# mLSTM: q and k copied with their 64-partition blocks exchanged, each score product split over both 64-row groups and two PSUM banks

## The reference, cut to what matters

```python
s = jnp.exp(d_log - m_t[..., None]) * jnp.einsum('bclhd,bcshd->bchls', qc, kc)
num = jnp.einsum('bchls,bcshv->bclhv', s, vc) + ...
den = jnp.sum(s, axis=-1) + ...
```

## Time and profile before

| what | us |
|---|---|
| runs shown | 3657.66, 3667.47, 3668.46 |
| median of them | 3667.47 |
| the profiled execution, its own time | 3659.06 |
| its span in the trace | 3657.3 |
| first product of layer 0 to the end of its last head | 339.47 to 463.48 |
| first product of layer 1 to the end of its last head | 2279.09 to 2375.73 |

### The profile page before, as it was taken

How to read it: one execution, slowest core, us unless ns; L and a number is a source line. 1 busy time by engine, 2 the same in 40 slices (tenths; PEclk the granted TensorE clock), 3 DMA queues, 4 the chain that set the end, 5 groups by cost and what they waited for, 6 DMA issues and landing times.

```text
span 3657.3 us, 70414 instructions
## 1 busy us (share of the span) xinstructions
PE 3407.7 (93%) x29874; PEld 2310.7 (63%) x29874; DVE 1172.9 (32%) x2555; ACT 707.3 (19%) x1346; POOL 104.0 (3%) x167
## 2 busy tenths in 40 slices
PE   7889999999999999999999989998999999999998
PEld 4456757678765777776777656666677665444444
DVE  1443415335624211111111453425264242222222
ACT  2313312122222100000001432320132201111111
POOL 0000100000000000000000000100000000000000
PEclk9999999999999999999999999998999999999999
DMA  5511020010034999999999401020201269999997
GB/s 214 231 53 52 24 81 12 29 53 30 30 121 173 350 362 374 361 355 364 362 362 356 169 2 66 33 81 12 81 30 56 106 255 410 415 416 416 417 414 292
DMA packets 100570, 733.01 MB, mean 200 GB/s; under 512 B 7888, under 2 KB 14160, under 8 KB 58336
## 3 DMA queue, kind: packets, MB, share of 16 engines
q1 hardware_dynamic: 90512, 692.54, 48.1%
q0 software_dynamic: 9808, 36.75, 3.3%
HBM read 710.34 MB, written 18.92 MB: 199 GB/s over the span
## 4 chain that ended last, share of the span: by engine, by line
PE 69%; DMA 19%; DVE 6%; ACT 3%; issue 2%; DVEq 0%; POOL 0%; SPq 0%; ACTq 0%; POOLq 0%
PE psum L654 14%; DMA ring<-in_w_e_gate 9%; PE psum L1199 8%; PE psum L546 8%; PE psum L1190 6%; DMA ring<-in_w_e_up 5%; PE psum L539 5%; PE psum L1231 4%; PE psum L1052 4%; PE psum L656 3%; DMA ring<-in_w_ada 2%; PE psum L776 2%; PE psum L1237 2%; DVE work L1944 2%; DMA ring<-in_w_e_down 2%
## 5 line engine op out<-in xcount | busy, mean ns | idle before, releaser
L654 PE MATMUL psum<-HT,ring 128*128 128x256 f32 x2560 | 614.9, 395 | 19.9 <-DVEq L2046 8.6
L654 PEld LDWEIGHTS psum<-HT,ring 128*128 128x128 f32 x2560 | 499.2, 198 | 117.1 <-issue 26.4
L1199 PE MATMUL psum<-work,ring 128*64 128x96 f32 x11264 | 486.2, 247 | 45.6 <-issue 30.7
L1199 PEld LDWEIGHTS psum<-work,ring 128*64 128x64 f32 x11264 | 471.1, 137 | 62.6 <-issue 44.7
L1430 ACT ACTIVATE work<-psum,small 128x768 f32<-128x768 f32 (+4 forms) x208 | 146.2, 703 | 700.7 <-PE psum L1237 327.1
L546 PE MATMUL psum<-ring,HT 128*128 128x512 f32 (+1 forms) x768 | 276.0, 521 | 0.0
L1190 PE MATMUL psum<-ring,work 128*64 128x256 f32 x1024 | 244.0, 393 | 30.0 <-DMA ring<-in_w_e_gate 28.1
L1191 PE MATMUL psum<-ring,work 128*64 128x256 f32 (+1 forms) x1024 | 238.0, 372 | 0.0
L1433 ACT ACTIVATE work<-psum 128x256 f32<-128x256 f32 (+7 forms) x219 | 103.5, 473 | 654.2 <-PE psum L546 237.8
L1231 PE MATMUL psum<-ring,work 128*64 128x512 f32 x960 | 220.3, 598 | 6.7 <-DMA ring<-in_w_e_down 6.4
L546 PEld LDWEIGHTS psum<-ring,HT 128*128 128x128 f32 x768 | 145.8, 190 | 127.3 <-issue 120.5
(11 more groups left out here) (229 smaller groups left out, 3791.7 us busy)
## 6 DMA issues: line engine op xcount, KB each, us to landing
ring<-in_w_e_gate SPq DMA_DIRECT2D x64, 2048.0 KB, 13.0
ring<-in_w_e_up SPq DMA_DIRECT2D x48, 2048.0 KB
ring<-in_w_e_down SPq DMA_DIRECT2D x48, 2048.0 KB
ring<-in_w_ada SPq DMA_DIRECT2D x24, 2048.0 KB, 11.7
ring<-in_w_e_up SPq DMA_DIRECT2D x32, 1536.0 KB, 11.0
ring<-in_w_gate SPq DMA_DIRECT2D x16, 2048.0 KB, 8.2
HT<-in_w_e_up SPq DMA_DIRECT2D x16, 2048.0 KB
ring<-in_w_e_gate SPq DMA_DIRECT2D x16, 1536.0 KB
```

Source lines behind the costliest of these rows:

```text
L654: pe.matmul(b[:, 0:256], w[:, k, d4 * P:(d4 + 1) * P], HT[:, k, off:off + 256], start=(k == 0), stop=(k == KD - 1))
L1199: ins = pe.matmul(b[lo:lo + 64, f * cap:(f + 1) * cap], w[:, k, c0:c0 + 64], e_xs[:, k, 0:cap], start=(k == 0), stop=(k == KD - 1))
```

## The change

`swap_head` copies, by two DMAs from POOL's queue for each head, the keys of a head and the last 384 columns of its queries into the other 64 partitions of a free area: for head 0 before the row copies, for heads 1 and 2 after the mask of item (0, 5), for head 3 after the mask of item (2, 1). `products` splits each item's queries into two halves. The first half uses the head's own row group; the second uses the exchanged copy in the other row group, except for items (0,0), (1,0), (3,0) and (3,1), where the copy is not used and both halves run in the own row group. Each half takes a bank of ring "d", which gets bank 2 (3, 4, 5, 2), so that one item has two banks that lie side by side; DVE reads both with one instruction where a direction covers the whole item. Ring "g" keeps banks 0 and 1 from the first product on; ahead of the products PE waits until four of the five first units are through DVE, and ahead of item (0,1) for the fifth. Cut to its core:

```diff
+        m_swap = [(gl_a, m_tmp[:, T // 2:T])] + [(m_sc[:, 0:T], m_sc[:, T:T + T // 2])] * 3
@@ mlstm on PE
                 ring("g", (0, 1, 2))
+                ring("d", (3, 4, 5, 2))
                 merge_units(L, ML_GAP)
...
                 quota = ml_quota(L)
+                gap = st["g"]
+                pe.wait_ge(sems["g_free"], gap - 1)
+                rings["g"].append((gap, (0, 1)))
 
                 def products(h, j):
-                    hp = (h % 2) * 64
-                    for off, n in (QS if j < CT else QS[:1]):
-                        b = job("d")
-                        pe.matmul(b[:, 0:n], m_qk[hp:hp + 64, 2 + h // 2, j * P:(j + 1) * P],
-                                       m_qk[hp:hp + 64, h // 2, off:off + n], start=True, stop=True).then_inc(sems["d_done"], 1)
+                    own, other = slice((h % 2) * 64, (h % 2) * 64 + 64), slice(64 - (h % 2) * 64, 128 - (h % 2) * 64)
+                    off, n = ml_span(L, j)
+                    n //= 2
+                    swapped = j >= (1, 1, 0, 2)[h]
+                    if swapped:
+                        pe.wait_ge(sems[f"ml_swap{h}"], 32 * (L + 1))
+                    b = job("d")
+                    pe.matmul(b[:, 0:n], m_qk[own, 2 + h // 2, j * P:(j + 1) * P],
+                              m_qk[own, h // 2, off:off + n], start=True, stop=True).then_inc(sems["d_done"], 1)
+                    off += n
+                    b = job("d")
+                    if swapped:
+                        keys, queries = m_swap[h]
+                        pe.matmul(b[:, 0:n], keys[other, j * P:(j + 1) * P], queries[other, off - T // 2:off - T // 2 + n],
+                                  start=True, stop=True).then_inc(sems["d_done"], 1)
+                    else:
+                        pe.matmul(b[:, 0:n], m_qk[own, 2 + h // 2, j * P:(j + 1) * P],
+                                  m_qk[own, h // 2, off:off + n], start=True, stop=True).then_inc(sems["d_done"], 1)
...
+                        if h == 0 and j == 0:
+                            pe.wait_ge(sems["g_free"], gap)
                         if j + 1 < NT:
                             products(h, j + 1)
...
                 merge_units(L, ML_END)
+                ring("d", (3, 4, 5))
                 finish_transposes(m_y)
@@ mlstm on DVE
+                        for x in range(2):
                             dve.wait_ge(sems["d_done"], c.nth("d_done"))
+                            bank()
+                        pair = (4, 2)[(h * NT + j) % 2]
+                        off, n = ml_span(L, j)
+                        n //= 2
+                        qk = psum[:, pair * 512:pair * 512 + 1024].rearrange("p (x t) -> p x t", x=2)[:, :, 0:n]
                         dve.wait_ge(sems["ml_mask"], c.nth("ml_mask"))
                         for d in range(2):
+                            for a, z in ml_runs(L, d, j):
+                                if (a, z) == (off, off + 2 * n):
+                                    w = m_W[:, j % 2, d, a:z].rearrange("p (x t) -> p x t", x=2)
+                                    stt(w, qk, 0.125, w, ALU.mult, ALU.mult)
+                                    continue
+                                for x in range(2):
+                                    lo, hi = max(a, off + x * n), min(z, off + x * n + n)
+                                    if lo < hi:
+                                        w = m_W[:, j % 2, d, lo:hi]
+                                        stt(w, qk[:, x, lo - off - x * n:hi - off - x * n], 0.125, w, ALU.mult, ALU.mult)
@@ POOL
+            def swap_head(h):
+                own, other = slice((h % 2) * 64, (h % 2) * 64 + 64), slice(64 - (h % 2) * 64, 128 - (h % 2) * 64)
+                keys, queries = m_swap[h]
+                pool.dma_start(keys[other, :], m_qk[own, 2 + h // 2, :]).then_inc(sems[f"ml_swap{h}"], 16)
+                pool.dma_start(queries[other, :], m_qk[own, h // 2, T // 2:T]).then_inc(sems[f"ml_swap{h}"], 16)
 
             def bring_rows(L):
+                pool.wait_ge(sems["ml_qk"], L + 1)
+                swap_head(0)
                 pool.wait_ge(sems["ml_m"], L + 1)
...
                         pool.sem_inc(sems["ml_mask"], 1)
+                        if (h, j) == (0, NT - 1):
+                            swap_head(1)
+                            swap_head(2)
+                        elif (h, j) == (2, 1):
+                            pool.wait_ge(sems["pv_done"], (L * 4 + 2) * NT)
+                            swap_head(3)
@@ module level
+def ml_span(L, j):
+    return (0, T) if L < DEPTH - 1 and j < CT else (CTX, LAT)
```

More of the change, by code:

```diff
@@ L199, in hybrid_layers @@
         names = ["dve_order", "act_order", "pool_order", "a_done", "a_free", "d_done", "d_free", "x_free", "row_free", "pv_done",
-                 "g_done", "g_free", "s_done", "s_free", "t_done", "t_free", "wbr0", "wbr1", "x_saved", "x_back", "ml_stored", "ml_bc0", "ml_bc1", "ml_bc2", "ml_bc3",
+                 "g_done", "g_free", "s_done", "s_free", "t_done", "t_free", "wbr0", "wbr1", "x_saved", "x_back", "ml_stored", "ml_swap0", "ml_swap1", "ml_swap2", "ml_swap3", "ml_bc0", "ml_bc1", "ml_bc2", "ml_bc3",
                  "const_in", "pack_in", "x_in", "w_in0", "w_in1", "w_in2", "w_ht", "w_xn0", "w_xn1", "w_half", "out_done", "x_new", "amod",
@@ L857, in mlstm @@
                 quota = ml_quota(L)
+                assert ML_GAP % 3 == 2 and quota[0] == 1
+                gap = st["g"]
+                pe.wait_ge(sems["g_free"], gap - 1)
+                rings["g"].append((gap, (0, 1)))
                 def products(h, j):
-                    hp = (h % 2) * 64
-                    for off, n in (QS if j < CT else QS[:1]):
-                        b = job("d")
-                        pe.matmul(b[:, 0:n], m_qk[hp:hp + 64, 2 + h // 2, j * P:(j + 1) * P],
-                                       m_qk[hp:hp + 64, h // 2, off:off + n], start=True, stop=True).then_inc(sems["d_done"], 1)
+                    own, other = slice((h % 2) * 64, (h % 2) * 64 + 64), slice(64 - (h % 2) * 64, 128 - (h % 2) * 64)
[16 more added lines that the diff above has]
+                                  m_qk[own, h // 2, off:off + n], start=True, stop=True).then_inc(sems["d_done"], 1)
                 for h in range(4):
@@ L2300, in mlstm @@
                     for j in range(NT):
-                        qk = {}
-                        for off, n in (QS if j < CT else QS[:1]):
+                        for x in range(2):
                             dve.wait_ge(sems["d_done"], c.nth("d_done"))
-                            qk[1 if off else 0] = bank()
+                            bank()
[3 more added lines that the diff above has]
+                        qk = psum[:, pair * 512:pair * 512 + 1024].rearrange("p (x t) -> p x t", x=2)[:, :, 0:n]
                         dve.wait_ge(sems["ml_mask"], c.nth("ml_mask"))
                         for d in range(2):
[L2307 to L2314, removed]
+                            for a, z in ml_runs(L, d, j):
[8 more added lines that the diff above has]
+                                        stt(w, qk[:, x, lo - off - x * n:hi - off - x * n], 0.125, w, ALU.mult, ALU.mult)
+                        for x in range(2):
                             dve.sem_inc(sems["d_free"], 1)
```

## The result

Twenty executions of each kernel: 3671.6 us after (median; 3662.59 to 3684.3) against 3663.18 before (3653.83 to 3672.21). The ratio is 1.0024, with an interval of 1.0014 to 1.0034: the change costs 8.8 us, between 5.1 and 12.5. I had forecast 1.5 us and called that no change.

A forecast was written before the change was run, and what follows sets the result against it. PE, busy 93% of the span, was taken to bound the kernel. Gains of 12.2 us against losses of 13.7 gave 3660.6 from 3659.1; run scatter put the forecast at 3665, range 3657 to 3673 (3652 to 3680 with rivals).

The forecast's parts named there:

- Halves side by side: mLSTM products: paired halves run together, 0.62 us per 256-column pair, 0.84 per 384; gains 8.8 us layer 0, 3.4 layer 1.
- A: mLSTM products: halves run one after the other, the 12.2 us gain is lost, 3677 us; chance 0.09.
- B: mLSTM products: each half's second pass holds up the other half, about 6 us of gain lost, 3671 us; chance 0.07.
- The waits: PE waiting for unit banks: start loses 0.65 us (layer 0) and 1.56 (layer 1), ends 4.57 and 2.05.
- Rival C: Stage start and end: clock holds and DVE's merge comes sooner, so the end costs less, 3657 us; chance 0.14.
- The clock at the start: Layer 0 opening: added idle time slows the first unit as in layer 1, 1.7 us lost, bounds 0 and 1.7.
- Its clock: Stage ends: the third last unit runs at lower clock after its wait, 2.4 us lost in layer 0, 0.8 in layer 1.
- Rival D: Layer 1 heads: more clock drops, units at j = 3 slow, 4 x 1.7 = 6.8 us, 3672 us; chance 0.12.
- DMAs, POOL, DVE: Copies and added DVE instructions cost nothing; landing 4.4 to 7.7 us as row loads, bound 1 us for the copies.

The follow-up runs named there:

- experiment 4: Changed kernel with both halves of every product in the head's own row group and no copies: 3685.68 us, ratio 1.0056 to the kernel before.
- Experiment 9: The kernel before, unedited, traced a second time: 3660.6 us over 12 executions, ratio 0.9993.
- experiment 1: Changed kernel with bank 2 given back to ring "g" for the last three units: 3657.6 us, ratio 0.9979 to the kernel before.
- experiment 2: Changed kernel with the wait for four merges moved from ahead of the first product to ahead of the first unit: 3666.49 us, ratio 1.0006.
- experiment 3: Changed kernel with bank 2 back for the last units and the first wait moved behind the first product: 3653.77 us, 0.9966 of the kernel before.
- experiment 5: Changed kernel with 10 (layer 0) and 4 (layer 1) unread matmuls ahead of the third last unit: 3664.63 us, 1.0001 of the kernel before.
- experiment 6: The kernel before with ring "g" cut to two banks for the last three units: 3671.09 us, ratio 1.0017.
- experiment 8: Experiment 3 plus four unread matmuls before item 5's wait in each head of layer 1: 3652.89 us, 0.9964 of the kernel before.

## Why the prediction was wrong

*Halves side by side: right.* 0.63 and 0.84 us for a pair were predicted as 0.62 and 0.84; the heads gained 8.5 us in layer 0 (8.8 predicted) and 4.0 in layer 1 (3.4). The second of these agrees in part by luck: in the third trace after it is 5.6, where one unit that opens a head in layer 1 ran slowly, against two in the first trace after and three before. Rivals A and B are refuted by the rows of the opening, where both groups start each pass together, and by experiment 4, which is what A would have been: 3685.68 us. B's rule of the Trainium skill ("TensorE: Matmul & The Clock Gate", section "The mechanism", starts and ends in program order) does not hold up the second half of a product here: the first passes of both groups start within 10 ns of one another, and so do the second passes.

*The waits: right.* 1.83 us at the start (1.78 predicted), 4.44 and 1.92 at the ends (4.57 and 2.05). Rival C, by which they would be smaller, is refuted.

*The clock at the start: the step that failed, with "Its clock" at the end.* I priced the start as the first unit of layer 1, 1.7 us, and set that as the upper bound. Measured from the small transposes to the first L904, the start lost 4.08 us, of which my wait terms explain 0.65; the clock cost 3.4, twice my upper bound (the other traces of the kernel before opened in 9.73 to 10.69 us, by which it is 2.3 at least). The row that I leant on held a unit of 5.41 us; here the product ahead of it runs slowly too (2.35 us instead of 1.49), and the unit takes 6.15. At the ends the losses are 7.7 and 3.9 us, of which 4.57 and 2.05 were the wait; that leaves 3.1 for the clock in layer 0, where I had 2.4, and 1.8 in layer 1, where I had 0.8. At the start of layer 1 I had 1.56 and the first two traces show 1.2, the third trace after 2.7. With these sizes my sum of 1.5 us becomes about 4.2, the difference of the first two traces' stages (258.0 against 253.8); by the means of all seven traces it is 3.4 (258.5 against 255.2). Of the 7.3 us by which the timed loss exceeds my sum, the stages with their mis-sized clock terms thus explain 1.9 to 2.7.

*The clock in GLA: not in the sum at all.* I followed each wait to its next unit and no further. In the traces after, GLA of layer 0 takes about 3.7 us longer up to the router, at a lower granted clock. With 3.4 to 4.2 that makes 7.1 to 7.9, against 8.8 (5.1 to 12.5) timed. That these come close proves little, since the stretches left out scatter by as much (by the means of the seven traces the experts of layer 0 are 7.2 us longer after, GLA of layer 1 0.7 and what follows it 2.1 shorter). Unit by unit, the longer GLA is one slow unit more: of the gate products in its first 110 us four take longer than 4.7 us in each trace of the changed kernel (in the first 5.51, 6.13, 5.12 and 6.16), and three, four, three and two in the four traces of the kernel before, none of the later ones behind a wait. Experiment 9, which has four, was 4.1 us behind the first trace of its own kernel after 159 us, as the changed kernel was after 88, and made 2.9 of that up later. The traces of experiments 1 to 6 had 520.3 to 522.0 there and experiment 8 had 524.3. Whether the change sets this, and how, is open: a wait at the end is not it, since experiment 6 has the wait and 520.3, and experiment 8 has no such wait and 524.3. A kernel that differs in nothing but when GLA begins was not tried.

*Rival D: refuted.* All units at j = 3 of layer 1 keep 3.72 us behind waits of about 0.9. *DMAs, POOL, DVE: right.* The copies' issue and landing, from the view of their second line, and nobody waits for them:

```profile
L2861 POOL DMA_DIRECT2D work<-work x8: 522/542/587, 320.2 to 2352.2; - x8
...
who waited for it (us, times):
...
DMA to landing us min/median/max: 2.5/2.6/4.1
```

The landing that I had bounded by the row loads, 7.7 us, was 4.1 at most.

## What to carry to other kernels

Before a bank is taken from one ring and given to another, look for the place where the first ring is used back to back behind a consumer that comes late, and give the bank back after its last use: that one line made this change 12.5 us faster than the kernel before, together with moving a wait behind the work that does not need it, where without them it was 8.8 us slower. Price a new wait on PE not by its length alone but with the clock that may fall behind it: a wait of 1.8 us, of which 0.65 us was left as lost time in the sum, cost 2.3 to 3.4 us more by the clock in the opening of layer 0. Where the wait can't go, work that nobody needs can get the clock's part back: it did so in the traced ends of experiment 5. And a sum of traced stages is worth checking against the stretches that nobody changed; here these moved by as much as the effect.

## What the runs showed of the hardware

- A wait of only 1.83 us on PE, behind the small transposes, was followed by a stretch at lower clock that cost more than the wait itself (granted clock 0.75 over 13.62 us). In the opening of layer 0 the first unit took 4.95 to 6.37 us in all six traces that wait there 1.83 us; with 0.26 us of waiting it took 3.72, 5.22 and 5.41 (experiments 2, 3, 8); in the kernel before and experiment 6, which do not wait there, 3.72 in four traces and 5.31 in one. So every trace with the wait has a slow unit there, but so have two of the three with 0.26 us and one without any.
- The length of a wait did not decide alone: in one trace a unit took 5.41 us behind 2.11 us and 3.72 behind 2.25, and units behind waits of 0.92 us kept 3.72.
- Matmuls into a bank that nobody reads, in place of a wait of 4.44 us, kept the next unit at 3.72 us instead of 6.67 (experiment 5).
- A stretch with the same instructions, the first 110 us of GLA in layer 0, ran at a granted clock of 0.89 in the changed kernel and in experiment 8 and of 0.91 to 0.95 in the kernel before; the difference lies in which of its units run slowly.
- Passes of fp32 matmuls in the two row groups start within 10 ns of one another although they stand one behind the other in the program, so that a product split over both costs 0.63 us against 1.06 for two halves in one group.
